# Head of the trunk kernel: what is fetched first, and in which order four slabs enter the first product

## The reference

```
h = _rmsnorm(x, e_norm_pre)              # x * rsqrt(mean(x*x) + 1e-6) * g
p = h @ w_in                             # 2048 x 7168
a_x, a_b, a_c, a_z, b_val, b_gate, b_z = split(p, 7)
ya = a_b * causal_conv3(a_c * a_x)
yb = silu(layernorm(causal_conv31(b_val * sigmoid(b_gate)) + bias))
x  = x + _rmsnorm(concat([ya * silu(a_z), yb * silu(b_z)]) @ w_out, e_norm_post)
# odd layer: a second mixer (window means, a map per group, gates), same norms
```

## Time and profile before

| | |
|---|---|
| median of the runs | 1307.91 us (1307.6 to 1308.23) |
| profiled execution | 1307.34 us, span 1305.5 us |
| PE busy | 1295.1 us, 99% of the span |
| DVE, ACT, POOL busy | 1018.6, 528.8, 142.4 us |
| moved by DMA | 254.39 MB, mean 195 GB/s |

### The profile page before, as it was taken

How to read it: one execution, slowest core, us unless ns; L and a number is a source line. 1 busy time by engine, 2 the same in 40 slices (tenths; PEclk the granted TensorE clock), 3 DMA queues, 4 the chain that set the end, 5 groups by cost and what they waited for, 6 DMA issues and landing times.

```text
span 1305.5 us, 17052 instructions
## 1 busy us (share of the span) xinstructions
PE 1295.1 (99%) x7006; PEld 1128.1 (86%) x7006; DVE 1018.6 (78%) x979; ACT 528.8 (41%) x595; POOL 142.4 (11%) x129
## 2 busy tenths in 40 slices
PE   9999999999999999999999999999999999999997
PEld 7888888888888888888888889999999999888886
DVE  6489999999955645444985899957888888899788
ACT  6521213213131212223555667654444445455452
POOL 0000000000006700000000110101213332000000
PEclk9999999999999999999999999999999999999999
DMA  9736677666567888862685576864344435674157
GB/s 325 228 92 199 162 229 232 193 185 190 166 188 217 257 266 279 243 198 87 236 312 193 178 208 210 281 189 121 114 122 125 136 112 169 251 242 144 54 204 258
DMA packets 260085, 254.39 MB, mean 195 GB/s; under 512 B 5488, under 2 KB 212464, under 8 KB 255024
## 3 DMA queue, kind: packets, MB, share of 16 engines
q1 hardware_dynamic: 253984, 243.03, 59.3%
q10 hardware_dynamic: 4512, 5.42, 1.3%
q0 software_dynamic: 1520, 4.98, 1.0%
HBM read 214.87 MB, written 38.54 MB: 194 GB/s over the span
## 4 chain that ended last, share of the span: by engine, by line
PE 99%; DMA 0%; DVE 0%; ACT 0%; DVEq 0%; issue 0%; SPq 0%; ACTq 0%
PE bank L1031 33%; PE bank L1033 33%; PE bank L1035 33%; PE bank L1067 1%; DMA raw<-e_in 0%; DVE rows L2541 0%; PE bank L1118 0%; PE bank L1105 0%; PE bank L1131 0%; PE bank L1125 0%; DVE w_lo L1887 0%; DVEq L151 0%; ACT w_hi L1387 0%; DVE rows L2173 0%; ACT junk L1518 0%
## 5 line engine op out<-in xcount | busy, mean ns | idle before, releaser
L1031 PE MATMUL bank<-h_hi,w_hi 128*128 128x512 f32 (+1 forms) x1472 | 520.2, 353 | 0.3 <-DVE w_lo L1887 0.3
L1033 PE MATMUL bank<-h_lo,w_hi 128*128 128x512 f32 (+1 forms) x1472 | 518.5, 352 | 0.0
L1035 PE MATMUL bank<-h_hi,w_lo 128*128 128x512 f32 (+1 forms) x1472 | 518.4, 352 | 0.0
L1031 PEld LDWEIGHTS bank<-h_hi,w_hi 128*128 128x128 f32 x1472 | 278.6, 189 | 38.7 <-issue 1.3
L1033 PEld LDWEIGHTS bank<-h_lo,w_hi 128*128 128x128 f32 x1472 | 278.7, 189 | 37.8 <-issue 0.7
L1035 PEld LDWEIGHTS bank<-h_hi,w_lo 128*128 128x128 f32 x1472 | 278.6, 189 | 37.5
L1845 DVE TENSOR_TENSOR w_lo<-raw,w_hi 128x2048 fp32r<-128x2048 f32 x60 | 148.4, 2473 | 33.7 <-ACT w_hi L1360 32.8
L1031 PE MATMUL bank<-w_hi,h_hi 128*128 128x512 f32 x448 | 174.5, 389 | 0.0
L1035 PE MATMUL bank<-w_hi,h_lo 128*128 128x512 f32 x448 | 174.3, 389 | 0.0
L1033 PE MATMUL bank<-w_lo,h_hi 128*128 128x512 f32 x448 | 174.3, 389 | 0.0
L1360 ACT ACTIVATE w_hi<-raw 128x2048 fp32r<-128x2048 f32 x60 | 113.9, 1908 | 93.6 <-PE bank L1035 66.4
(11 more groups left out here) (175 smaller groups left out, 1479.7 us busy)
## 6 DMA issues: line engine op xcount, KB each, us to landing
raw<-e_in SPq DMA_DIRECT2D x52, 1024.0 KB, 5.9
scratch<-e_out SPq DMA_DIRECT2D x17, 1024.0 KB, 7.4
scratch<-o_in SPq DMA_DIRECT2D x24, 512.0 KB, 7.6
pair_sums<-scratch SPq DMA_DIRECT2D x24, 512.0 KB, 6.5
spare<-e_out SPq DMA_DIRECT2D x12, 1024.0 KB, 7.6
rows<-o_in SPq DMA_DIRECT2D x24, 512.0 KB, 4.2
spare<-o_out SPq DMA_DIRECT2D x12, 1024.0 KB, 6.5
raw<-o_in SPq DMA_DIRECT2D x22, 512.0 KB, 4.2
```

Of the source, the lines that this page charges most:

```text
L1031: nc.tensor.matmul(dst, w[0], m[0], start=first, stop=False, skip_group_check=goes_on)
L1033: nc.tensor.matmul(dst, w[0], m[1], start=False, stop=False, skip_group_check=goes_on)
L1035: return nc.tensor.matmul(dst, w[1], m[0], start=False, stop=last, skip_group_check=goes_on)
```

## The change

SP fetches x tile 0 and then, in one transfer of 128 KB, k tile 0 of slabs 0 and 1 (into a free place in `scratch`); then x tile 1, the other three k tiles of the first quarter of slabs 0 and 1 (192 KB each), and the first quarters of slabs 2 and 3 (also into `scratch`), and only then x tiles 2 and 3 and the rest in the old order. The 16 columns of `vecs` with the gains come first and alone; the other 328 are issued by ACT behind the first quarters. x pairs 4 and 5, and pairs 6 and 7, now share a semaphore each, on which ACT waits for 32, that is for both pairs. PE takes k tiles 0 and 1 of slabs 0 and 1, then the same of slabs 2 and 3, then k tiles 2 and 3 of all four, then k tiles 4 to 15 as before. POOL clears two rows of `scratch` later, since the first tiles lie there.

```
+FIRST_TILE, FIRST_REST = (0, 1), (1, QUARTER)
+FIRST_PIECES = [*((q, *FIRST_TILE) for q in range(2)), *((q, *FIRST_REST) for q in range(2)),
+                *((q, *FIRST_QUARTERS[0]) for q in range(2, 4)),
+                *((q, *FIRST_QUARTERS[j]) for j in range(1, 4) for q in range(2)),
+                *((q, *FIRST_QUARTERS[j]) for q in range(2, 4) for j in range(1, 4))]
...
+        def x_load(pair):
+
+            return pair if pair < 4 else pair // 2 + 2
...
             load_x(slice(0, 1), x_first_loaded)
-            for j in range(4):
-                if j > 0:
-                    load_x_pair(2 * j)
+            load_first_tiles()
+            load_x(slice(1, 2), x_loaded[0])
+            for n in range(RAW):
+                load_first(n, 0, *FIRST_REST)
+            load_first_quarters()
+            load_x_pair(1)
+            for j in range(1, 4):
+                load_x_pair(2 * j)
                 for n in range(RAW):
-                    load_first(n, j)
-                if j == 0:
-                    load_x(slice(1, 2), x_loaded[0])
+                    load_first(n, j, *FIRST_QUARTERS[j])
                 load_x_pair(2 * j + 1)
             for n in range(RAW):
-                for j in range(4):
+                for j in range(1, 4):
                     if j < 3:
-                        sp.wait_ge(first_lo, RAW * j + n + 1)
+                        sp.wait_ge(first_lo, first_lows(n, *FIRST_QUARTERS[j]))
                     else:
                         sp.wait_ge(lo_ready, n + 1)
-                    load_first(RAW + n, j)
+                    load_first(RAW + n, j, *FIRST_QUARTERS[j])
...
-            for k in range(KT):
+            for k in range(2):
                 pe.wait_ge(x_lo_ready, k + 1)
                 for q in range(RAW):
                     first_product(q, k)
+            for k in range(2):
+                for q in range(RAW, SLOTS):
+                    first_product(q, k)
+            for k in range(2, KT):
+                pe.wait_ge(x_lo_ready, k + 1)
+                for q in range(SLOTS if k < QUARTER else RAW):
+                    first_product(q, k)
             for q in range(RAW, SLOTS):
-                for k in range(KT):
+                for k in range(QUARTER, KT):
                     first_product(q, k)
...
-            act.dma_start(vecs[:, :], vec).then_inc(vec_loaded, 16)
+            pre = AT_VEC["pre"]
+            act.dma_start(vecs[:, pre:], vec[:, pre:]).then_inc(pre_loaded, 16)
...
+            for q in range(RAW, SLOTS):
+                first_split(q, *FIRST_QUARTERS[0])
+            act.dma_start(vecs[:, 0:pre], vec[:, 0:pre]).then_inc(vec_loaded, 16)
+            for k in range(2, KT):
+                if k % 2 == 0:
+                    act.wait_ge(x_loaded[x_load(k // 2)], 32 if k >= KT // 2 else 16)
+                x_rounded(k)
+                if k > QUARTER and k % QUARTER == 1:
+                    for q in range(RAW):
+                        first_quarter_split(q, k // QUARTER)
+            for q in range(RAW, SLOTS):
+                for j in range(1, 4):
+                    first_quarter_split(q, j)
```

More of the change, by code:

```diff
@@ L260, in build @@
         x_first_loaded = sem("x_first_loaded")
-        x_loaded = [sem(f"x_loaded{p}") for p in range(KT // 2)]
+        x_loaded = [sem(f"x_loaded{n}") for n in range(6)]
         x_tok_loaded = [sem(f"x_tok_loaded{n}") for n in range(2)]
@@ L362, in build, with first_raw, first_lows @@
         gain_next_loaded = sem("gain_next_loaded")
+        def first_raw(q, start, end):
+            if (start, end) == FIRST_TILE:
+                return first_tile[:, 1 - q, :]
+            if q >= RAW and start == 0:
+                return first_quarter[:, SLOTS - 1 - q, :]
+            return raw[:, q % RAW, start * P:end * P]
+        def x_load(pair):
+            return pair if pair < 4 else pair // 2 + 2
+        def first_lows(q, start, end):
+            n = FIRST_PIECES.index((q, start, end))
+            return sum(1 for piece in FIRST_PIECES[:n + 1] if piece[2] < KT)
         def f32(ap):
@@ L526, in load_x_pair, with load_first, column_pair, load_first_tiles @@
             def load_x_pair(pair):
[L528 to L535, removed]
+                load_x(slice(2 * pair, 2 * pair + 2), x_loaded[x_load(pair)])
+            def load_first(q, j, start, end):
+                sp.dma_start(first_raw(q, start, end).rearrange("p (k c) -> p k c", c=P),
+                             columns(e_in, E1A_ORDER[q])[:, start:end, :])\
+                    .then_inc(first_loaded[q % RAW][j], 16)
+            def column_pair(first, apart):
+                return e_in.rearrange("(k p) n -> p k n", p=P)[:, :, first:first + apart + P]\
+                    .rearrange("p k (n c) -> p n k c", c=P)[:, ::apart // P]
+            def load_first_tiles():
+                pair = column_pair(B_VAL, B_GATE - B_VAL)
+                sp.dma_start(first_tile, pair[:, :, 0, :]).then_inc(first_tile_loaded, 16)
+            def load_first_quarters():
+                pair = column_pair(A_X, A_C - A_X)
+                for n in range(2):
+                    sp.dma_start(first_quarter[:, n, :].rearrange("p (k c) -> p k c", c=P),
+                                 pair[:, n, 0:QUARTER, :]).then_inc(first_quarter_loaded, 16)
             def load_tokens(t):
@@ L1078, in first_product @@
             def first_product(q, k):
-                if k % QUARTER == 0 and k < 3 * QUARTER:
-                    j = k // QUARTER
-                    pe.wait_ge(first_lo, RAW * j + q + 1 if q < RAW else 3 * q + j + 1)
-                elif k % QUARTER == 0:
-                    pe.wait_ge(lo_ready, q + 1)
+                for piece in FIRST_PIECES:
+                    if piece[0] == q and piece[1] == k and piece[2] < KT:
+                        pe.wait_ge(first_lo, first_lows(*piece))
+                    elif piece[0] == q and piece[1] == k:
+                        pe.wait_ge(lo_ready, q + 1)
                 last = product(bank[4 + q][:, :], weights(q, k, P), operand(k),
@@ L1381, in x_rounded, with first_split, first_quarter_split @@
                                      scale=col("pre", k)).then_inc(x_hi_ready, 1)
-            def first_split(q, j):
+            def first_split(q, start, end):
+                nc.scalar.activation(w_hi[:, q, start * P:end * P], first_raw(q, start, end),
+                                     ACT.Copy).then_inc(first_hi, 1)
+            def first_quarter_split(q, j):
                 act.wait_ge(first_loaded[q % RAW][j], 16 * (q // RAW + 1))
-                part = slice(j * T, (j + 1) * T)
-                nc.scalar.activation(w_hi[:, q, part], raw[:, q % RAW, part], ACT.Copy)\
-                    .then_inc(first_hi, 1)
+                first_split(q, *FIRST_QUARTERS[j])
             def x_square(t):
```

74 lines of the change are left out of this document (44 added, 30 removed).

## The result

The changed kernel took 1310.4 us, median of 20 runs (1309.61 to 1312.64); the kernel before, on the same chip, 1307.95 us, median of 20 (1307.46 to 1309.62). The ratio is 1.002, 95% interval 1.0013 to 1.0026: slower by 2.5 us (1.7 to 3.4 by the interval). Forecast were 1308.8 us and a range of 1307.0 to 1309.9, so the direction was right and the size fell outside. The profiled execution took 1310.38 us and has a span of 1308.5 us (before 1307.34 and 1305.5), at a mean granted clock of 0.999.

A forecast was written before the change was run, and what follows sets the result against it. PE was taken as the bound, so only its start and waits count. A 2.4 us pause less 1.81 spare, plus 0.13 and a 0.2 restart, gave +0.9, the start's gain being swallowed: 1308.8 us, range 1307.0 to 1309.9.

The forecast's parts named there:

- a wait for the diagonals: At the spreading matmul: PE asks at 55.27, diagonals are ready at 56.6, so PE waits 1.4 us; chance 0.65.
- the hole: In the DMA stream near 25 to 27 us: SP's queue waits for slab 0's last rest, leaving loads paused.
- Term B, the pause: Loads behind SP's blocked queue, token blocks included, come 2.4 us later, the middle of 1.9 to 3.0.
- Term A, the start: First product bound by the warm-up's end at 6.29, not data; PE gains 0.33 to 0.76 us, swallowed later.
- The wait at slab 2's first quarter: At k tile 0 of slabs 2 and 3, near 9.01 us: PE waits 0 to 0.4 us, swallowed later.
- The sum: At the spreading matmul: the late diagonals, net of spare time, make the kernel 0.9 us slower.
- The clock rival: At the diagonals: a PE wait of 3 us or more drops the clock, costing 1.5 us more; chance 0.06.
- Tokens in time: At the diagonals: pause under 1.05 us, no PE wait, the start's gain kept, 1307.1 to 1307.9 us; chance 0.25.

The follow-up runs named there:

- 5: Changed kernel with a semaphore for each x pair and whole 256 KB first quarters of slabs 0 and 1: 1307.75 us, ratio 0.9996.
- 1: Changed kernel with a semaphore for each x pair again, nothing else moved: 1308.88 us, ratio 1.0004.
- 6: Kernel before with only the 16 gain columns fetched first, the other 328 issued behind x tile 3: 1307.98 us, ratio 0.9999.
- 7: Kernel before with the gains first and PE's warm-up started earlier, on the matrix of ones: 1308.54 us, ratio 1.0003.
- 11: The changed kernel, unaltered, executed once more for its profile: 1311.11 us.
- 10: Changed kernel with the diagonals made behind the rest of slab 6 instead of ahead of it: 1314.62 us, ratio 1.0047.
- 8: Kernel before with the shared semaphores for x pairs 4 and 5, and 6 and 7, alone: 1310.6 us, ratio 1.0019.
- 9: Changed kernel with a semaphore per x pair, whole first quarters, and two token blocks issued ahead of slab 2's last quarter: 1307.75 us, ratio 0.9996.
- 2: Changed kernel, semaphores still shared, with the first two token blocks issued ahead of slab 2's last quarter: 1308.61 us, ratio 1.0006.
- 4: Changed kernel's start alone: gains and small first tiles ahead, a semaphore per x pair, slabs 2 and 3 in the old order; 1308.5 us, ratio 1.0004.
- 3: Changed kernel with both a semaphore per x pair and the first two token blocks issued ahead of slab 2's last quarter: 1308.73 us, ratio 1.0005.
- 12: Kernel before with the shared semaphores alone, executed once more for its profile: 1312.95 us.

## Why the prediction was wrong

The chain of reasons held: the place (a wait for the diagonals), the releaser, the length of the wait (1.4 us forecast, 1.49 measured), the hole (forecast near 25 to 27 us, measured from about 25.5 to 28.7), and no wait behind it. Two terms were mis-sized, and since the wait is the difference of the two, its right length is luck: both were off the same way.

**Term B, the pause: 2.4 us forecast (1.9 to 3.0), 4.67 measured.** This is the step that failed. The prediction put it between 1.9 us (by landings) and 3.0 (by bytes) and took the middle. By landings, in the rows of ACT above, slab 2's last quarter comes 3.63 us later than the fourth last quarter of before (30.82 against 27.19), the first token block 5.00 (37.13 against 32.13), the last 4.67. So landings did not catch up as the lower end had it; between that quarter and the first token block another 1.4 us were lost, which had no term. Read off by the last token block, along the kernels that lie between before and after:

| kernel | last token block squared from | step |
|---|---|---|
| before | 47.30 us | |
| quarters of slabs 2 and 3 ahead, with PE's new order (5) | 48.80 us | +1.50 |
| and small first transfers (1) | 50.27 us | +1.47 |
| and shared semaphores (after) | 51.97 us | +1.70 |

Each row is one execution, and executions scatter: with the same loads, experiments 6 and 7 have 48.64 and 47.41 us; the changed kernel has 51.97 and, in 11 and 10, 52.16 and 51.53; the kernel of 8 has 50.61 and 52.90. The first step can't be told from this scatter. The other two are borne out by run times, 1.2 us (5 against 1) and 1.7 us (1 against after).

- The quarters put ahead of the x pairs: x pair 7 was to land 1.8 us later by its bytes. In experiments 5 and 9 it was rounded from 24.37 and 23.60, 2.7 and 2.0 us later than at 21.63; the token block moved by 1.5 or 1.6.
- The small transfers had no price in the prediction; it took 311 GB/s for the first 20 us and measured were 292, with 76 and 137 GB/s from 3.5 to 4.5 us where before had 299 and 323. The quarters of slabs 2 and 3 were split from 9.50, not from 7.6 to 8.0; in the six profiles with the small transfers and this order it is 9.11 to 9.80, in the two without 8.20 and 8.40.
- The shared semaphores: the prediction followed pair 7 and k tile 12 only, from 23.4. Measured were 24.88, 1.5 us later, some of it there without the small transfers (24.37 in 5); the rest done at 27.7, not 26.2, and the hole ended near 28.7, not 27.2. By itself this edit costs 2.2 us of time in the kernel before (8) and 1.7 here. It is the largest single cost by run times.

**Term A, the start: 0.33 to 0.76 us forecast, 0.76 taken, 0.15 measured.** The data were in time, as the step had it: the first product starts behind the warm-up without a wait. It even starts at 5.95, before the modelled end of the warm-up at 6.29 that the step took as its bound. What was missed is that the 0.88 us over the first two steps in the earlier trace rows were for the most part not a restart, which goes with the wait, but the lower clock: behind a wait two steps at the upper level take 0.53 (20.78 to 21.31 in experiment 8). The first matmuls run at 0.43 us start to start until the clock comes up, at 7.80 here; before it was about 7.3. Starting sooner puts more matmuls on the slow side of that moment. This moment is not the kernel's own, though: the 7th matmul starts at 7.84 in the second execution of the changed kernel, where the clock was up at 6.9. And where the clock was up by the first products (1, 2, 4, 10), the 7th matmul waits 0.4 to 0.9 us for the rest of k tile 1's weights and starts at 8.03 to 8.22. In the seven profiles with this start the 7th matmul lies between 0.6 us earlier and 0.2 later than before's 8.42, and in the four-slab order none of it lasts: the 13th matmul, slab 2's first, waits for its weights whenever PE gets there.

**The wait at slab 2's first quarter: 0 to 0.4 us forecast, 1.10 measured** (1.8 in a second execution). It goes with the thin stream: the wait is gone where the small transfers are (5, 9). That a stall there is swallowed by the one at the diagonals was right for the changed kernel: experiments 1, 2 and 3 take away the wait for the diagonals, and 0.5 to 0.8 us stay above before.

**The sum.** PE asked at 57.45 (58.94 - 1.49) instead of 55.27. Slab 2's first matmul, forecast for 9.01 to 9.4, starts at 10.91, and the 13th matmul of before at 9.79; so PE lies 1.12 behind before there and not 0.76 ahead, which is 1.88 of the 2.18; 0.30 lie spread behind it. This lateness cost nothing by itself, since the diagonals came later still. The diagonals were done at 58.89 instead of 56.6, and 58.94 - 56.03 = 2.9 us came out instead of 0.9.

One smaller slip: the prediction lets a landing that is 0.3 us faster move term B by 0.3. It moves only the lower end, and so the middle by 0.15. (Behind the hole a quarter landed 3.1 us after its issue, where the prediction used 2.9.)

**The clock rival** was given 0.06 and put from a wait of 3 us on. Its price was right: experiment 10 has a wait of 3.5 us and 1.7 us of clock, where 1.5 was forecast. Its threshold was not. It rested in part on the earlier trace rows, where the clock stands at 1.00 through 2.5 us of idleness at the start; but the trace has no clock record before 7.3 us, and the first two steps of PE in the earlier trace rows are those of the lower level, so that 1.00 says nothing of the clock. And the clock fell behind waits of 1.8 us (4) and 1.9 us (12), and did not behind ones of 1.9 us (8) and of 1.1, 1.5 and 1.8 us (the two executions of the changed kernel). No length of wait separates these. In 5 of its 20 runs the changed kernel took 1311.87 to 1312.64 us, 1.9 above the others, and their mean clock is 0.997 where the profiled one has 0.999. That fits such a fall, but no profile of one was had, so for this kernel it is argued, not shown. The Trainium skill (TensorE: Matmul & The Clock Gate, The HAM clock gate) has idleness as what closes the gate; the rows agree, with the addition that in two of the three cases here the level changed after PE was at work again.

"Tokens in time" (0.25) needed a pause of less than 1.05 us and failed by the 4.67. The shared semaphore, which stood against it in the text, is not all of it: in experiments 1 and 2, with the cause or the effect of the sharing taken out, the tokens were in time, but the last block still came 2.97 and 2.15 us later than before, and PE, held at slab 2, asked at 57.59 and 56.89 instead of 55.27.

**A version that beats both?** Experiments 5 and 9 have the lowest medians, 1307.75 us each, 0.45 and 0.67 below before's on their chips. Both intervals (0.9987 to 1.0005) hold 1, so they beat the changed kernel and are not told from before. All 22 of their runs lie below before's median on their chip, which hints at a gain of some tenths. Little is left at this end of the kernel: in their profiles PE's list has 0.3 us at the first product or nothing.

## What to carry to other kernels

A wait that is widened from one load to two moves everything that is queued behind it on that engine, and then all that the freed buffers let go: follow it for each such wait, not only for the last one, and price it alone before it is packed with others. Ahead of a saturated stream a few small transfers are not free for their bytes; here three of 128 to 192 KB cost 1.2 us. A start that is moved forward by some tenths is worth nothing when the next product waits for its data, and little while the clock is still at its lower level: compare start-to-start distances with 0.23 us before a slow pair of matmuls is put down to a wait. And when two profiles of kernels with the same loads differ by more than a microsecond at the row that you read, a step of that size between two kernels needs the runs' times beside it.

## What the runs showed of the hardware

- The time at which TensorE first ran at its upper level differed from execution to execution although the warm-up was the same: by the trace's clock records 5.4 us in experiment 4, 5.7 in 5, 7.3 before, 7.8 and 6.9 in the two executions of the changed kernel, 8.6 in experiment 3; and 10.2 with the gap behind the warm-up (7). Where products run by then, their start-to-start distance changes from 0.43 to 0.23 us there.
- Each time the clock fell while PE had work left it stayed at half for about 3.4 us, 1.7 us of work, in three kernels (4, 10, 12). In two of them (4, 12) it fell 0.7 and 1.5 us after PE had restarted; in the third (10) at the restart.
- Small transfers back to back at the head of the stream: in the changed kernel 76 and 137 GB/s over half a microsecond each, at a DMA share of 0.47 and 0.84, against 299 and 323 GB/s before, with 256 KB ones.
- SP's issue takes longer behind many transfers: the two last quarters of slabs 0 and 1, which wait for no semaphore, took it 3.51 us (from 13.62), the two first, of 192 KB each, 0.96 (from 2.17). That its queue was full is our reading. Early on an issue takes 0.42 us for 128 KB and 0.46 for 256 KB, so small transfers also put fewer bytes into the queue in the same time; that this is the cause of the thin stream was not tested.
